# Head norm of an RWKV/Fourier mixer: one root and reciprocal per channel tile on six gathered rows

## What is computed

```python
    o = o_f + o_b
    mu = jnp.mean(o, axis=-1, keepdims=True)
    var = jnp.mean(jnp.square(o - mu), axis=-1, keepdims=True)
    o = (o - mu) * lax.rsqrt(var + GN_EPS) * heads(lnx_w.astype(f32)) + heads(lnx_b.astype(f32))
    bonus = jnp.sum(jnp.sum(r_h[:, :, None] * k_dir * r_k.astype(f32), axis=-1, keepdims=True)
                    * v_h[:, :, None], axis=2)
    o = (o + bonus).reshape(B, T, RWKV_WIDTH) * g
    y_rwkv = o.astype(h.dtype) @ w_o_rwkv
    y_four = fourier_mix(f, grid) @ w_fourier
```

## Time and profile before

| what | us |
|---|---|
| runs, median (3 runs) | 2978.11 |
| runs, lowest and highest | 2973.72, 2978.93 |
| the profiled execution, its own time | 2980.43 |
| its span in the trace | 2978.6 |
| first product of head_norm (L2184) starts | 1770.19 |
| Fourier input `fo_f` on the chip, PE starts on it | 1784.83 |
| ACT starts on the Fourier stage (L2396) | 1846.60 |
| PE starts on the Fourier stage's large products (L2386) | 1850.97 |
| PE starts on `merge` (L948) | 1885.31 |

### The profile page before, as it was taken

The page is one execution under the profiler, slowest core; times in us unless marked ns, Lnnn a source line. Parts: engine busy times, 40 slices in busy tenths (PEclk is TensorE's granted clock), DMA queues, the critical chain, the costliest instruction groups (busy, mean ns, idle before and its releaser), DMA issues. The chain is left out here.

```text
span 2978.6 us, 53460 instructions
## 1 busy us (share of the span) xinstructions
PE 2812.2 (94%) x21936; PEld 2680.6 (90%) x21936; DVE 1541.9 (52%) x2777; ACT 805.3 (27%) x1409; POOL 468.7 (16%) x561
## 2 busy tenths in 40 slices
PE   7999999999998999999689977899899999999998
PEld 4999999999997988899578865899799999999997
DVE  4456665666536355632477758455633333333335
ACT  4211111111115233444155545221511111111111
POOL 4101001110005001222233324122500000000001
PEclk9999999999999999999799999999999999999999
DMA  6122222222202423444655423312111111111112
GB/s 270 57 71 85 71 84 85 85 76 79 65 13 103 144 101 129 142 140 159 176 118 117 100 95 124 121 67 67 36 41 41 40 41 39 41 41 42 42 43 71
DMA packets 187198, 257.67 MB, mean 87 GB/s; under 512 B 99072, under 2 KB 136960, under 8 KB 185376
## 3 DMA queue, kind: packets, MB, share of 16 engines
q1 hardware_dynamic: 173280, 227.86, 23.6%
q0 software_dynamic: 12608, 27.48, 2.9%
q10 hardware_dynamic: 1152, 0.07, 0.0%
HBM read 200.23 MB, written 55.12 MB: 86 GB/s over the span
## 5 line engine op out<-in xcount | busy, mean ns | idle before, releaser
L845 DVE SCALAR_TENSOR_TENSOR x<-bank,gate,x 128x128 f32<-128x128 f32 (+1 forms) x832 | 409.6, 515 | 199.9 <-PE bank L963 199.3
L1014 ACT ACTIVATE act_out_ffn<-bank 128x384 f32<-128x384 f32 x132 | 64.9, 492 | 1267.8 <-PE bank L948 1267.8
L1017 DVE TENSOR_TENSOR g_ffn<-act_out_ffn,bank 128x384 f32<-128x384 f32 x132 | 73.2, 554 | 616.6 <-ACT act_out_ffn L1014 616.6
L948 PE MATMUL bank<-h_hi_ffn,wlo_a_ffn 128*128 128x384 f32 x1056 | 358.8, 340 | 11.3 <-DVE h_lo_ffn L663 4.5
L948 PE MATMUL bank<-h_lo_ffn,whi_a_ffn 128*128 128x384 f32 x1056 | 356.4, 338 | 0.0
L948 PE MATMUL bank<-h_hi_ffn,whi_a_ffn 128*128 128x384 f32 x1056 | 356.2, 337 | 0.0
L948 PE MATMUL bank<-h_hi_ffn,whi_b_ffn 128*128 128x384 f32 x1056 | 354.9, 336 | 0.0
L948 PE MATMUL bank<-h_lo_ffn,whi_b_ffn 128*128 128x384 f32 x1056 | 354.9, 336 | 0.0
L948 PE MATMUL bank<-h_hi_ffn,wlo_b_ffn 128*128 128x384 f32 x1056 | 354.9, 336 | 0.0
L963 PE MATMUL bank<-g_hi_ffn,wlo_d_ffn 128*128 128x384 f32 x1056 | 354.0, 335 | 0.0
L963 PE MATMUL bank<-g_lo_ffn,whi_d_ffn 128*128 128x384 f32 x1056 | 352.8, 334 | 0.0
(11 more groups left out here) (300 smaller groups left out, 4924.9 us busy)
## 6 DMA issues: line engine op xcount, KB each, us to landing
ada_beside_ffn<-in_ada_w POOLq DMA_DIRECT2D x96, 256.0 KB, 3.6
raw_a_ffn<-in_ffn_w SPq DMA_DIRECT2D x44, 512.0 KB, 4.4
raw_b_ffn<-in_ffn_w SPq DMA_DIRECT2D x44, 512.0 KB, 5.0
raw_d_ffn<-in_ffn_w SPq DMA_DIRECT2D x44, 512.0 KB, 3.7
raw_in<-in_w_in SPq DMA_DIRECT2D x35, 512.0 KB, 5.3
mix<-row_out SPq DMA_DIRECT2D x23, 576.0 KB, 3.1
sc_ar<-streams SPq DMA_DIRECT2D x36, 256.0 KB, 3.7
gates<-mix SPq DMA_DIRECT2D x16, 576.0 KB, 5.2
```

What stands on the lines that cost most here:

```text
L845: ins = nc.vector.scalar_tensor_tensor(xs, kit.banks[4 + d % 4][:, a:b], kit.gate[:, gate, d, cond:cond + 1], xs, ALU.mult, ALU.add)
L948: mm = nc.tensor.matmul(kit.banks[2 * slot + j][:, 0:CH], w[q][:, par, cols], v[:, k, toks], start=(k == 0 and m == 0), stop=(k == ku - 1 ...
L1014: return self.nc.scalar.activation(out, a, ACT.Silu)
L1017: self.nc.vector.tensor_tensor(g32, act_out, b, ALU.mult).then_inc(g32_ready, 1)
```

## The change

Instead of leaving each head's variance on all 64 of its partitions, PE now gathers it in rows. The weights of `variance` are a 128x6 matrix `pick`, one for each chunk c, that is zero but for the columns 2c and 2c+1, which hold the ones of the two heads. The three chunks of a channel tile accumulate into one region of six rows by 384 columns in bank 7. ACT takes one root of this region and DVE one reciprocal, both 6x384, per channel tile. PE `spread` then multiplies by `back`, the transpose of `pick` for the chunk, which lays the two rows of the chunk back on 128 partitions in bank 6, and DVE multiplies `o` by it out of PSUM. `pick` is set by DVE at the start, transposed by PE and copied by ACT to `back`.

The banks are dealt anew: the gate's product has bank 2 alone, `spread` bank 6, the Fourier pieces bank 3, the rows bank 7. So `gate`, `spread` and `channels` each wait for the reader of the step just before. The lags of what follows the variance grow.

The diff, cut to its core:

```diff
-        "f_in", "dft_in", "g_done", "g_ready")}
+        "f_in", "dft_in", "g_done", "g_ready", "blank", "picked", "turned", "rows_ready", "spread_done")}
...
+        ROWS = 2 * NC
+        pick, back = buf("hn_pick", [P, NC, ROWS]), buf("hn_back", [ROWS, NC, P])
+        roots, inv = buf("hn_roots", [ROWS, 2, CH]), buf("hn_inv", [ROWS, 2, CH])
...
-        waves_bank = lambda u: kit.banks[4 * (u % 2) + 3]
+        waves_bank, gate_bank, spread_bank, rows_bank = (kit.banks[q] for q in (3, 2, 6, 7))
+
+        whole = lambda m: m % NC == NC - 1
...
             def sums(m):
                 if m >= 2:
-                    pe.wait_ge(s["rooted"], m - 1)
+                    pe.wait_ge(s["centered"], m - 1)
                 nc.tensor.matmul(bank(m, 0), cst.pair_ones, at(o, m), start=True, stop=True).then_inc(s["mean_done"], 1)
 
             def variance(m):
+                ct, c = divmod(m, NC)
                 pe.wait_ge(s["squared"], m + 1)
-                nc.tensor.matmul(bank(m, 0), cst.pair_ones, at(r, m), start=True, stop=True).then_inc(s["var_done"], 1)
+                if c == 0:
+                    pe.wait_ge(*((s["rooted"], ct) if ct else (s["rows_ready"], 1)))
+                ins = nc.tensor.matmul(rows_bank[0:ROWS, 0:CH], pick[:, c], at(r, m), start=(c == 0), stop=whole(m))
+                if whole(m):
+                    ins.then_inc(s["var_done"], 1)
+
+            def spread(m):
+                ct, c = divmod(m, NC)
+                pe.wait_ge(s["inverted"], ct + 1)
+                if m:
+                    pe.wait_ge(s["scaled"], m)
+                nc.tensor.matmul(spread_bank[:, 0:CH], back[:, c], inv[:, ct % 2], start=True, stop=True)\
+                    .then_inc(s["spread_done"], 1)
...
             def gate(m):
-                if m >= 2:
-                    pe.wait_ge(s["gated"], m - 1)
-                elif m == 0:
+                if m:
+                    pe.wait_ge(s["gated"], m)
+                else:
                     pe.wait_ge(s["loaded"], 32)
...
-                if u >= 2:
-                    pe.wait_ge(s["g_ready"], u - 1)
-                out = waves_bank(u)
+                if u:
+                    pe.wait_ge(s["g_ready"], u)
+                out = waves_bank
...
-            skewed([(0, sums), (1, bonus), (1, variance), (2, gate), (2, channels)])
+
+            pe.wait_ge(s["picked"], NC)
+            for c in range(NC):
+                ins = nc.tensor.transpose(rows_bank[0:ROWS, c * P:(c + 1) * P], pick[:, c], cst.ident)
+            ins.then_inc(s["turned"], 1)
+            skewed([(0, sums), (1, bonus), (1, variance), (5, spread), (6, gate), (2, channels)])
...
             def root(m):
...
+                act.wait_ge(s["var_done"], ct + 1)
+                if ct >= 2:
+                    act.wait_ge(s["inverted"], ct - 1)
+                nc.scalar.activation(roots[:, ct % 2], rows_bank[0:ROWS, 0:CH], ACT.Sqrt, scale=1.0 / HD,
+                                     bias=kit.eps[0:ROWS, 1:2]).then_inc(s["rooted"], 1)
...
-            skewed([(0, square), (1, root), (2, channels), (2, affine), (3, high)])
+            act.wait_ge(s["turned"], 1)
+            nc.scalar.activation(back[:].rearrange("r c p -> r (c p)"), rows_bank[0:ROWS, 0:NC * P], ACT.Copy)\
+                .then_inc(s["rows_ready"], 1)
+            skewed([(0, square), (1, root), (2, channels), (6, affine), (7, high)])
...
+            def inverse(m):
+                if whole(m):
+                    ct = m // NC
+                    dve.wait_ge(s["rooted"], ct + 1)
+                    nc.vector.reciprocal(inv[:, ct % 2], roots[:, ct % 2]).then_inc(s["inverted"], 1)
+
             def normed(m):
-                dve.wait_ge(s["rooted"], m + 1)
-                nc.vector.reciprocal(at(kd_sum, m), at(r, m)).then_inc(s["inverted"], 1)
-                dve.wait_ge(s["inverted"], m + 1)
-                nc.vector.tensor_tensor(at(o, m), at(o, m), at(kd_sum, m), ALU.mult).then_inc(s["scaled"], 1)
+                dve.wait_ge(s["spread_done"], m + 1)
+                nc.vector.tensor_tensor(at(o, m), spread_bank[:, 0:CH], at(o, m), ALU.mult).then_inc(s["scaled"], 1)
...
-            skewed([(0, center), (2, bonus), (3, gated), (1, normed)])
+            nc.vector.memset(pick[:], 0.0).then_inc(s["blank"], 1)
+            dve.wait_ge(s["blank"], 1)
+            for c in range(NC):
+                nc.vector.tensor_copy(pick[:, c, 2 * c:2 * c + 2], cst.pair_ones[:, 0:P:HD]).then_inc(s["picked"], 1)
+            skewed([(0, center), (2, inverse), (2, bonus), (7, gated), (5, normed)])
...
-            skewed([(0, weighted), (2, with_bonus), (3, low)])
+            skewed([(0, weighted), (6, with_bonus), (7, low)])
...
-                if q < 3:
-                    pe.wait_ge(prev.s[("rooted", "bonus_v", "gated")[q]], prev.steps)
+                pe.wait_ge(prev.s[("centered", "bonus_v", "scaled", "rooted")[q]], CT if q == 3 else prev.steps)
```

More of the change, by code:

```diff
@@ L2198, in gate @@
             def gate(m):
-                if m >= 2:
-                    pe.wait_ge(s["gated"], m - 1)
-                elif m == 0:
+                if m:
+                    pe.wait_ge(s["gated"], m)
+                else:
                     pe.wait_ge(s["loaded"], 32)
-                nc.tensor.matmul(bank(m, 2), g_up[:, ct_of(m) * P:(ct_of(m) + 1) * P], gd[:, part(m)],
+                nc.tensor.matmul(gate_bank[:, 0:CH], g_up[:, ct_of(m) * P:(ct_of(m) + 1) * P], gd[:, part(m)],
                                  start=True, stop=True).then_inc(s["gate_done"], 1)
@@ L2237, in root @@
             def root(m):
-                act.wait_ge(s["var_done"], m + 1)
-                nc.scalar.activation(at(r, m), bank(m, 0), ACT.Sqrt, scale=1.0 / HD, bias=kit.eps[:, 1:2])\
-                    .then_inc(s["rooted"], 1)
+                if not whole(m):
+                    return
+                ct = m // NC
[4 more added lines that the diff above has]
+                                     bias=kit.eps[0:ROWS, 1:2]).then_inc(s["rooted"], 1)
             def affine(m):
@@ L2254, in channels @@
                 act.wait_ge(s["g_done"], u + 1)
-                src = waves_bank(u)
+                src = waves_bank
                 if u < 2:
@@ L2286, in gated @@
                 dve.wait_ge(s["gate_done"], m + 1)
-                nc.vector.tensor_tensor(at(o, m), bank(m, 2), at(v, m), ALU.mult).then_inc(s["gated"], 1)
-            skewed([(0, center), (2, bonus), (3, gated), (1, normed)])
+                nc.vector.tensor_tensor(at(o, m), gate_bank[:, 0:CH], at(v, m), ALU.mult).then_inc(s["gated"], 1)
+            nc.vector.memset(pick[:], 0.0).then_inc(s["blank"], 1)
[3 more added lines that the diff above has]
+            skewed([(0, center), (2, inverse), (2, bonus), (7, gated), (5, normed)])
         def gpsimd(pool):
```

## The result

| | before | changed |
|---|---|---|
| median | 2978.11 us (5 runs, 2971.02 to 2978.93) | 2991.31 us (5 runs, 2988.07 to 2993.87) |
| profiled execution | 2980.43 us, span 2978.6 | 2990.26 us, span 2988.5 |

The ratio is 1.0042, interval 1.003 to 1.0055: slower by more than 0.2%, and outside the range of 2974 to 2988. The forecast was 2981.6. The page's first part answers the earlier trace rows.

What follows compares the result with a forecast made beforehand. The stage before the Fourier products was taken as bound by a ring through ACT's and POOL's queues, not DVE. Longer drain and later PE entry cost +2.7 to +4.3, middle +3.5: 2978.11 + 3.5 = 2981.6 us, range 2974 to 2988.

Steps and rivals of the forecast that it cites:

- The ring: Loop through ACT's and POOL's in-order queues in full turns: from 5.47 us a turn to 4.68, 5.15 with a root.
- DVE was the bound after all: Rival, chance 0.08: fewer reciprocals let full turns run at PE's 4.3 us, total -8 us, 2970.
- The lock: DVE's product with two SBUF inputs and POOL's weighted shut each other out; its end takes weighted from 1.32 to 1.00 us.
- The six-row reciprocal: DVE's reciprocal on six partitions, taken as 2.55 us, with bounds of 0.2 and 2.55.
- The rival that it is short: Rival, chance 0.24 together with a faster fill: short six-row reciprocal, -1.3 us, 2976.8.
- The second ring: Single gate bank makes gate wait for the previous gated: 4.5 to 4.6 us, 6.65 with the reciprocal ahead of gated.
- the filling: Turns 2 to 5, without affine under the longer lags; first affine, of turn 6, forecast at 1803.9.
- Turn 10: Full turn with the reciprocal again ahead of gated on DVE, part of it covered: 6.1 us.
- the rival's mechanism: PE drops to half clock after waiting 2.3 us behind gated, at the gates of turns 7 and 10; chance 0.18.
- the one on draining: Last steps: POOL's with_bonus and low, 0.96 us each, set the pace; ACT enters the Fourier stage 1.6 us later.
- The half-clock rival: Half clock in turns 7 and 10 and once in the drain adds 5 to 10 us, about 2989; chance 0.18.

Runs made afterwards that it cites:

- e5_psum: The kernel before, all 12 full reciprocals kept, with the reciprocal written to PSUM and gate waiting for its product; 2977.32 us, ratio 0.9987 to 1.0004.
- e11_after: The changed kernel itself run once more, in the same rounds as e12_tall; 2989.95 us, ratio to before 1.0026 to 1.0053.
- e1_tall: The changed kernel with the inputs of spread filled with zeros to 128 rows; 2981.22 us, ratio to before 1.0004 to 1.0023.
- e12_tall: The same program as e1_tall run again, beside the changed kernel; 2980.57 us, ratio to before 1.0005 to 1.0025.
- e2_behind: The changed kernel with the six-row reciprocal issued behind gated on DVE; 2989.48 us, ratio to before 1.0024 to 1.0048.
- e4_two: The changed kernel with gates alternating between two banks again and the sums in one; 2980.85 us, ratio to before 0.9998 to 1.0017.
- e6_tall_two: The changed kernel with spread's inputs zero-filled to 128 rows and two gate banks; 2976.05 us, ratio to before 0.9984 to 1.0001.
- e8_tall_behind: The changed kernel with spread's inputs zero-filled to 128 rows and the reciprocal behind gated on DVE; 2981.54 us, ratio to before 1.0 to 1.0022.
- e3_fill: The changed kernel with an unused 128-row product ahead of each gate in the last six turns; 2986.59 us, ratio to before 1.002 to 1.0039.

## Why the prediction was wrong

Up to turn 12 most of its terms hold.
- *The ring.* Forecast 4.68 a plain turn and 5.15 with a root, measured 4.75 and 5.15. DVE is in none of the waits of a plain turn, and e5_psum shortened its turns by 0.2 to 0.3 us with all 12 reciprocals in place. So "DVE was the bound after all" (0.08) fell.
- *The lock.* Taken 1.00 us for `weighted`, measured 1.00, and 1.00 by itself in e5_psum. The Trainium skill (SBUF — State Buffer, "Who interferes with whom") says that a DVE instruction with at most one SBUF input, outside the modes that use both ports, does not contend with GpSimd; the traces agree, with 1.00 us in place of 1.32.
- *The six-row reciprocal.* Taken 2.55, measured 2.53. The rival that it is short fell.
- *The second ring.* Turn 7 was put at 6.65 and took 6.42. The first affine was put at 1803.9 and came at 1804.45, though the stage had begun 0.6 us sooner than before, so the filling was 1.2 us longer than forecast.
- *Turn 10* was put at 6.1 and took 7.57, half of it at half clock, as the rival's mechanism and place had it. That is 1.5 us.

**The step that failed** is the one on draining: POOL makes with_bonus and low in pairs, 0.96 each from start to start, "and nothing else is slower". At half clock spread and gate took 1.57 us each, 3.15 a step against POOL's 1.91. The last gate came at 1851.11, not 1845.85, and the large products at 1862.33, not at 1854.5 to 1856.1. I had costed the six-row products by their columns alone and never asked what they do to the clock. For their length that is nearly right: at full clock the next product starts 0.84 us after a six-row spread and 0.75 after one of 128 rows.

Cut at three points, the stage shows where the time went (us):

| | to the affine of turn 12 | to the last gate | to the first large product | to merge |
|---|---|---|---|---|
| forecast | 65.64 | 10.05 | 8.65 to 10.25 | |
| changed | 68.31 | 13.28 | 11.15 | 32.98 |
| e11_after | 68.32 | 12.74 | 11.27 | 33.68 |
| e1_tall | 65.85 | 10.07 | 9.52 | 34.38 |
| e12_tall | 67.22 | 10.08 | 7.60 | 33.42 |

The changed kernel's stage grew by 10.6 us where 3.5 were forecast. Of the 7 us between, 3.2 are the drain's steps, 0.9 to 2.5 the small products behind them, still at half clock at first, and 2.7 lie ahead of the drain, 1.5 of them in turn 10; the last part gave 1.4 back against the kernel before (34.34). The rows of spread explain the drain: with 128 of them it takes 10.07 and 10.08 us, as forecast. They do not explain turn 10, whose fall came with 128 rows too. With zero rows the kernel is the one that the prediction worked out: 2981.22 and 2980.57 us against 2981.6 forecast, a stage of 119.82 and 118.32 against 118.65. That both totals lie so close is in part luck, since e12_tall lost 1.4 us in turn 10 and won about 2 in the handover.

The half-clock rival (0.18, about 2989) gave nearly the measured time, and that is luck in good part. It put two of its three stretches into turns 7 and 10, and only one of these came, for 1.5 us; the drain it put at one stretch of 3.3 to 6.6 us, and the clock was down there for about 10. It rested on waits of over 2 us behind gated. e12_tall has such a wait at the drain's entry (2.30 us) and keeps its clock. The Trainium skill (TensorE: Matmul & The Clock Gate, "HAM oscillation — how this bites in real kernels") tells of a kernel whose matmuls wait for data in every turn of its loop, longer than they work, and fall to the half clock each time. No run here tests that: PE's waits in e12_tall's drain are 2.30 us once, then 0.36 a step and 1.00 ahead of the last gate, and the clock stayed 1.00 from 1836 to 1852. A chance of 0.18 was too small on other grounds as well: the rows before showed one such fall in the handover, and the change lengthened the handover.

What stays open: why turn 10 falls in some executions and not in others, and whether the variance products, now 128 rows high but six columns wide, have a part in it; the 1.7 to 3 us of the medians that are in no trace; and the worth of the reciprocal's place by itself.

## What to carry to other kernels

A product with few contraction rows took about as long here as a full one and still cost the clock. Where such products make up much of PE's work beside its waits, look at the granted clock there, and fill both inputs with zero rows, which cost two memsets here. Relief on an engine outside the ring that sets a turn is worth nothing, while longer lags lengthen the drain, and the drain is where each added product stands alone on the path. When a bank is given up to make room, list whose wait it shortens by one step, and what long instruction now stands in that wait.

## What the runs showed of the hardware

- The clock: two programs with the same products and the same order, one with 6 and one with 128 rows in 12 of its products. In e11_after PE was busy 4.00 of 4.00 us at a clock of 0.52, in e12_tall 2.68 of 4.00 at 1.00 in the same stretch. The engine that was busier had the slower clock.
- Coming back: while PE alternated six-row and full products, its clock stayed at 0.50 to the last gate in four executions of four (the changed kernel, e11_after, e2_behind, e4_two). With 128 rows it came back in the drain in both that had fallen (e6_tall_two and e8_tall_behind).
- The reciprocal of 384 fp32 columns takes 2.53 us on 6 rows, 2.55 on 128, and 2.56 written to PSUM.
- With an unused full product ahead of each gate the granted clock was 0.80 and 0.78 in the first two windows of e3_fill's drain, and 1.00 from 1844.
